# Walking every second output tile's row blocks backwards in a feed-forward loop

## The reference

```python
def swiglu_ffn(x, w_gu, w_down):          # x: tokens x 1024
    gu = x @ w_gu                         # 1024 x 5632
    gate, up = jnp.split(gu, 2, axis=-1)  # 2816 each
    return (jax.nn.silu(gate) * up) @ w_down   # 2816 x 1024
```

## Time and profile before

| | |
|---|---|
| median of three executions | 2073.41 us (2072.38 to 2075.15) |
| the profiled execution, its own time | 2074.92 us |
| its span, first to last instruction | 2073.1 us |
| mean granted TensorE clock | 0.998 |
| TensorE busy | 2042.4 us (99%) |
| TensorE weight loads busy | 2031.4 us (98%) |
| VectorE busy | 1181.7 us (57%) |
| ScalarE busy | 679.8 us (33%) |
| GpSimd busy | 72.2 us (3%) |

### The profile page before, as it was taken

The page is one execution under the profiler, slowest core; times in us unless marked ns, Lnnn a source line. Parts: engine busy times, 40 slices in busy tenths (PEclk is TensorE's granted clock), DMA queues, the critical chain, the costliest instruction groups (busy, mean ns, idle before and its releaser), DMA issues. The chain is left out here.

```text
span 2073.1 us, 34481 instructions
## 1 busy us (share of the span) xinstructions
PE 2042.4 (99%) x13041; PEld 2031.4 (98%) x13041; DVE 1181.7 (57%) x2365; ACT 679.8 (33%) x1401; POOL 72.2 (3%) x112
## 2 busy tenths in 40 slices
PE   7999999999999999999999999999999999999998
PEld 7999999999999999999999999999999999999997
DVE  5643554354435579537886855344534453458977
ACT  5321222122212234316874532211221222124555
POOL 0000000000000002321000000000000000000000
PEclk9999999999999999999999999999999999999999
DMA  5171111011101101322121211011101110120213
GB/s 169 61 108 35 61 61 37 24 61 61 40 20 61 61 1 51 70 57 50 47 83 62 82 62 61 10 51 61 61 10 51 61 61 10 51 81 20 85 41 105
DMA packets 153277, 116.17 MB, mean 56 GB/s; under 512 B 72648, under 2 KB 143628, under 8 KB 153200
## 3 DMA queue, kind: packets, MB, share of 16 engines
q1 hardware_dynamic: 117728, 108.41, 16.9%
q10 hardware_dynamic: 33424, 5.67, 2.0%
q0 software_dynamic: 2048, 1.06, 0.3%
HBM read 105.96 MB, written 9.15 MB: 56 GB/s over the span
## 5 line engine op out<-in xcount | busy, mean ns | idle before, releaser
L860 PE MATMUL ps<-x_hi,w_lo 128*128 128x352 f32 x2688 | 882.8, 328 | 6.3 <-DVE x_lo L2183 2.1
L862 PE MATMUL ps<-x_hi,w_hi 128*128 128x352 f32 x2688 | 862.7, 321 | 0.0
L861 PE MATMUL ps<-x_lo,w_hi 128*128 128x352 f32 x2688 | 862.5, 321 | 0.0
L860 PEld LDWEIGHTS ps<-x_hi,w_lo 128*128 128x128 f32 x2688 | 505.5, 188 | 9.1 <-DVE x_lo L2183 3.3
L861 PEld LDWEIGHTS ps<-x_lo,w_hi 128*128 128x128 f32 x2688 | 506.4, 188 | 0.0
L862 PEld LDWEIGHTS ps<-x_hi,w_hi 128*128 128x128 f32 x2688 | 504.6, 188 | 0.0
L860 PE MATMUL ps<-a_hi,wd_lo 128*128 128x352 f32 x1104 | 356.9, 323 | 0.4 <-DVE a_lo L2248 0.4
L861 PE MATMUL ps<-a_lo,wd_hi 128*128 128x352 f32 x1104 | 353.8, 320 | 0.0
L862 PE MATMUL ps<-a_hi,wd_hi 128*128 128x352 f32 x1104 | 353.7, 320 | 0.0
L2296 DVE TENSOR_TENSOR acc<-ps,acc 128x352 f32<-128x352 f32 x480 | 250.4, 523 | 83.7 <-PE ps L862 77.7
L2231 DVE TENSOR_TENSOR tmp_u<-ps,rstd_pre 128x352 f32<-128x352 f32 x132 | 69.0, 524 | 337.0 <-PE ps L862 337.0
(11 more groups left out here) (225 smaller groups left out, 1566.1 us busy)
## 6 DMA issues: line engine op xcount, KB each, us to landing
raw<-in_ffn_w_gu_dram SPq DMA_DIRECT2D x88, 512.0 KB, 3.5
rawd<-in_ffn_w_down_dram SPq DMA_DIRECT2D x22, 1024.0 KB, 6.9
raw<-in_w_in_dram SPq DMA_DIRECT2D x16, 512.0 KB, 4.0
raw<-in_w_out_dram SPq DMA_DIRECT2D x16, 512.0 KB, 3.9
raw<-in_ple_w_gate_dram SPq DMA_DIRECT2D x16, 512.0 KB, 3.6
toeplitz<-rev ACTq DMA_DIRECT2D x8, 512.0 KB, 8.3
x_in<-in_x_prompt_dram SPq DMA_DIRECT2D x4, 512.0 KB, 9.4
toep_first<-toeplitz SPq DMA_DIRECT2D x32, 64.0 KB, 2.2
```

The source lines that it names most:

```text
L860: eng.matmul(dst, wl, xh, start=first, stop=False)
L861: eng.matmul(dst, wh, xl, start=False, stop=False)
L862: return eng.matmul(dst, wh, xh, start=False, stop=last)
```

## The change

Inside the two hardware loops, the gate/up tiles and the down tiles are made by new functions, which go through a tile's row blocks forwards in even tiles and backwards in odd ones. `k == order[0]` opens the accumulation and `k == order[-1]` closes it. Steps 0 and 10 and everything outside the feed-forward loops keep the functions that they had.

```diff
+            def there_and_back(f, i, off, n, ks, weights, rows):
+
+                bank_at(i * STEP, off)
+                order = list(range(ks)) if n % 2 == 0 else list(range(ks))[::-1]
+                for k in order:
+                    mm = passes(ps[:, off % BANKS, 0:C], *weights(k), *rows(k),
+                                k == order[0], k == order[-1])
+                mm.then_inc(psum_full, 1)
+
+            def gate_turns(f, i, c):
+
+                for t in range(4):
+                    s, h = SPECS[t]
+                    if c == 0 and h == 0:
+                        wide_ready(f, i, s)
+                    there_and_back(f, i, gate_tile(f, i, c, t), t, KT, lambda k: wide(s, k, h),
+                                   lambda k: (x_hi[:, k, cols(c)], x_lo[:, k, cols(c)]))
+
+            def down_turns(f, i, c):
+
+                eng.wait_ge(a_lo_done, i * (NC * G) + (NI * NC * G * f + 2 * c + 2))
+
+                def part(t, m):
+                    sl = slice(t * D + m * P, t * D + m * P + P)
+                    return wd_hi[:, sl], wd_lo[:, sl]
+
+                for m in range(KT):
+                    there_and_back(f, i, down_tile(f, i, c, m), m, G, lambda t: part(t, m),
+                                   lambda t: (a_hi[:, t, cols(c)], a_lo[:, t, cols(c)]))
+
             def ffn_step(f, i):
 
                 for c in range(NC):
-                    gate_products(f, i, c)
+                    gate_turns(f, i, c)
                 down_ready(f, i)
                 for c in range(NC):
-                    down_products(f, i, c)
+                    down_turns(f, i, c)
```

## The result

| | before | changed |
|---|---|---|
| median of 13 executions | 2073.09 us (2072.38 to 2075.15) | 2078.46 us (2077.02 to 2081.94) |
| ratio, with its 95% interval | | 1.0027 [1.0019, 1.0035] |
| span of the profiled execution | 2073.1 us | 2076.2 us |

The change makes the kernel slower by 0.27%, 5.4 us. The forecast was no change, 2073.4 us in a range of 2070.8 to 2075.9; the result lies above it.

What follows compares the result with a forecast made beforehand. TensorE was taken to bound the kernel. The profiled 2073.1 us span + 1.82 us around it + 0 for the change gave 2074.9 us, or 2073.4 us as the median; range 2070.8 to 2075.9 us.

Steps and rivals of the forecast that it cites:

- rival (c): In the loops, a late VectorE read-out or missed weight half adds a wait: 7.2 us, 2080.6 us; chance 0.015.
- Steps of 68.66 us that repeat exactly: Each iteration of the first hardware loop takes 68.66 us, nine making 617.94 us, without variation.
- a step that moves by over 0.23 us: Sign that the prediction is wrong: a loop iteration's length on the timeline moves by over 0.23 us.
- what is left is the price of a switch: In the loops, waits and DMA change by zero, leaving only the cost of tile switches on the same rows, taken as 0.
- 540 x (price of one switch on the same rows): Loop term: 540 tile switches streaming the same rows, price taken as 0; 1.3 ns each would be 0.7 us.
- the projection's 70 intervals: Mixer's input projection, 806.21 to 817.35 us: 159.14 ns per matmul, 18 same-row switches costing at most 1.3 ns each.
- there is no toll at the place that the change edits: In the loops, switching tile costs below 1 ns over an ordinary step, from equal gate and down paces.
- Rival (b): At the loops' 540 switches, colliding reads of the same rows slow matmuls: 7.6 us, 2081.0 us, +0.4%; chance 0.03.
- Rival (a): At the loops' 540 switches, same rows are cheaper to stream again: up to 6.6 us saved, 2066.8 us; chance 0.035.
- The rule of the Trainium skill: Loop matmuls: a 149.2 ns floor for 352 columns would let switches give back at most 5.2 us.

Runs made afterwards that it cites:

- run 11: Kernel before, with only chunk 2's down tile 6 backwards in each step: 2072.67 us, ratio 1.0000.
- run 9: Kernel before, with odd gate/up tiles in block order 5, 0, 3, 4, 1, 2, 7, 6, no switch on the same rows: 2073.70 us, 1.0005.
- run 2: Changed kernel with gate/up tiles put back forward, so only the down tiles alternate: 2084.24 us, ratio 1.0057 to the kernel before.
- run 4: Kernel before, with only the last down tile of each step (chunk 2, tile 7) backwards: 2082.77 us, ratio 1.0046.
- run 12: TensorE alone, layer not computed: 40 streams of 96 matmuls at listed addresses; forward gate streams 158.9 or 161.1 ns a matmul, shifted weights up to 163.3.
- run 13: TensorE alone, layer not computed: six orders of the loop's step at its addresses, without waits; gate parts 45.76 to 46.32 us, the kernels' to 0.01 us.
- run 10: Kernel before, with the last down tile of each step backwards and chunk 0's gate tiles in order 1, 0, 3, 2, 5, 4, 7, 6: 2081.98 us, 1.0045.

## Why the prediction was wrong

**What held.** TensorE is the bound in the loops and each nanosecond between matmuls counts in full. No wait, clock or DMA moved: rival (c) is out, and nothing that the change does is undone by slack elsewhere. Steps of 68.66 us that repeat exactly were the right thing to read, and a step that moves by over 0.23 us was the right sign of a wrong forecast: it moved by 0.27.

**What failed** is the step headed "what is left is the price of a switch". It made the term 540 x (price of one switch on the same rows), with the price 0 from the projection's 70 intervals. The price of such a switch was read rightly: run 11 has two for 7 ns a step, and by run 9 even the small tolls don't need the same rows. But the sum assumed that a matmul's pace is a property of the matmul and that a new order can add or save only at the places where it differs. Runs 2 and 4 show a pace that belongs to the stream: which of several beats it is in depends on addresses and on what went before, and in run 4 it keeps a slow one for the 288 matmuls of a gate part, behind six reordered ones. So the term that was put at 0 measured 0.11 us a step in the down part and 0.17 in the gate part, 4.6 us in the two loops, and another 0.6 us in the two steps 10, which the change doesn't touch and the sum didn't have at all.

**The conclusion "there is no toll at the place that the change edits"** came from gate and down parts having one pace, 158.9 and 159.0 ns. That one number held for both because both were in the same beat, not because nothing else is possible. Before's trace has the counterexample. In the mixer's output projection TensorE waits for nothing from 1097.86 to 1125.59 us, and starts 173 matmuls of the same shape:

```profile
1097.86 0.33 PE L861 MATMUL ps<-y_lo,w_hi 128*128 128x352 f32 x1
...
1125.59 0.32 PE L862 MATMUL ps<-y_hi,w_hi 128*128 128x352 f32 x1
```

27.73 us in 172 distances are 161.2 ns, the slow beat of run 4, in the kernel before. It isn't the only one: from the starts of matmuls, 116 from 1004.46 us on come 161.3 ns apart, 176 from 1879.64 us on 160.7, and 170 from 1973.24 us on 159.9. Had I compared every stretch of 352-column matmuls instead of one, 2.3 ns on the 7776 matmuls of the two loops, or 18 us, would have been a bound above. I took the stretch that looked most like the switch and let it stand for the stream.

**Rival (b)** named the right side and a size near it, 7.6 us, by the wrong mechanism, and that is luck: no run shows a collision of two readings of the same rows at a switch. **Rival (a)** is out: no same-row switch saved anything, and holding rows and weights still in run 12 gave 160.0 ns, not less than 158.9. **The rule of the Trainium skill** in the forecast, a warm gap of N/2.4 + 2.5 ns for a matmul by itself ("TensorE: Matmul & The Clock Gate", section "Back-to-back issue gap"), gives 149.2 ns; the runs show 158.9, 160.0, 161.1 and up to 163.3 ns for this shape with a weight load ahead of each matmul. The Trainium skill's page "SBUF — State Buffer", section "Who interferes with whom", says that TensorE never waits on anyone and that its two read ports, for rows and for weights, are independent. The first part agrees with run 13, where the other engines' absence changed nothing. The second is hard to square with run 12, where moving the weights against the rows changes the pace; which of the two reads is held, if either is, no run shows.

**What stays open.** Why a backward tile 7 starts the slow beat and a backward tile 6, or all eight of chunk 2, don't, isn't settled; run 10 refuted my rule for it. That the reads of rows and of weights get in each other's way in SBUF would fit the change of pace with the addresses in run 12, but it is argued and not shown. In run 12 +256 bytes isn't as +0 and +512 is (158.9 against 161.1 and 161.1 ns), so 256 bytes isn't the whole period of it, if it has one. What keeps the past, which runs 4 and 13 show, wasn't tried. No order was found that is faster than before's: its loops already run in the best beat seen. Its slower stretches outside the loops were left alone; by the four paces above 158.9 ns, they hold some 1.2 us, an estimate.

## What to carry to other kernels

Where TensorE is full, compare the distance between starts over every long stretch of one shape before calling a reordering free: if two stretches differ, the pace can be a state of the stream, and a change of order or placement ahead of it can move it. Here six matmuls a step moved a gate part by 1.2%, and 64 bytes moved it by 0.7%. Judge such a change by the length of a repeated step rather than by busy shares, and if the length moves, undo it a tile at a time: the cause can stand in another part than the loss. A kernel that looks tuned may have been lucky in its addresses, so a harmless edit that costs 0.3 to 0.6% may be worth trying again with the tensors placed otherwise. That this gets the loss back is not shown: the one other placement tried made both orders equal, at a slower pace.

## What was unexpected in the hardware

- TensorE's stream of weight loads and 352-column matmuls has several stable paces at the 2.4 GHz clock level: 158.9, 160.0 and 161.1 ns a matmul in the kernels' loops, up to 163.3 ns in streams by themselves.
- One forward stream had two of them, 158.9 and 161.1 ns, with its weights moved by 256 and by 512 bytes, and in the kernel at one address after different predecessors.
- Six reordered matmuls of 432 cost 0.55 us of a 68.66 us step; a tensor of 64 bytes placed elsewhere made the step 0.38 us longer and the kernel 11.6 us of 2073, some 2.5 of them by a wait.
- Half of a change (run 2, +11.6 us) can cost twice the whole (+5.4 us).
- At the lower clock level the pace was the columns' alone, 293.3 ns; at the upper one it is 12 to 17 ns over their 146.7.
